# Gated sum and final norm on GpSimd and ScalarE, with another write-back plan, in a macaron decoder layer

## What is computed

```python
h = x
h = h + 0.5 * swiglu(rmsnorm(h, ffn1_norm), ffn1_w_gate, ffn1_w_up, ffn1_w_down)   # D_FF = 2816
u = rmsnorm(h, mix_norm)
a_val, a_gate, b_B, b_C, b_x, g_a, g_b = split(u @ w_in)                           # 7 x 1024 columns
a = silu(layernorm(causal_depthwise_conv(a_val * sigmoid(a_gate), 31 taps) + bias))
y_a = a @ a_w_out
y_b = (b_B * causal_depthwise_conv(b_C * b_x, 3 taps)) @ b_w_out
m = sigmoid(g_a) * y_a + sigmoid(g_b) * y_b
h = h + m @ w_o
h = h + 0.5 * swiglu(rmsnorm(h, ffn2_norm), ffn2_w_gate, ffn2_w_up, ffn2_w_down)
out = rmsnorm(h, final_norm)
```

## Time and profile before

| | us |
|---|---|
| runs: median (lowest to highest of 3) | 3187.16 (3183.77 to 3187.34) |
| profiled execution, its own time | 3187.8 |
| its span, slowest core (the 8: 3170.6 to 3186.2) | 3186.2 |
| PE busy | 3058.0 (96%) |
| DVE busy | 2464.7 (77%) |
| ACT busy | 872.9 (27%) |
| POOL busy (DMA issue only) | 191.1 (6%) |
| DMA moved | 618.14 MB, mean 194 GB/s |

### The profile page before, as it was taken

The page is one execution under the profiler, slowest core; times in us unless marked ns, Lnnn a source line. Parts: engine busy times, 40 slices in busy tenths (PEclk is TensorE's granted clock), DMA queues, the critical chain, the costliest instruction groups (busy, mean ns, idle before and its releaser), DMA issues.

```text
span 3186.2 us, 45381 instructions; the slowest of 8 cores (3170.6 to 3186.2 us)
## 1 busy us (share of the span) xinstructions
PE 3058.0 (96%) x14160; PEld 1386.8 (44%) x14160; DVE 2464.7 (77%) x3458; ACT 872.9 (27%) x1570; POOL 191.1 (6%) x363
## 2 busy tenths in 40 slices
PE   7988899999998999998999999999999999999997
PEld 2433344444443443443444444444444444444445
DVE  2268898869887697958898699989897899897332
ACT  1122233223321223313242233322421332232221
POOL 1111001000110000000000000000001000000000
PEclk9999999999999999999999999999999999999998
DMA  9999989988999779796565656554657545645454
GB/s 178 137 211 198 221 226 176 224 219 212 185 206 248 225 184 241 206 258 210 162 204 171 199 185 207 195 176 154 212 148 231 164 156 184 216 147 197 145 186 158
DMA packets 184649, 618.14 MB, mean 194 GB/s; under 512 B 21024, under 2 KB 23200, under 8 KB 178656
## 3 DMA queue, kind: packets, MB, share of 16 engines
q1 hardware_dynamic: 137024, 440.20, 43.9%
q0 software_dynamic: 45872, 172.78, 28.4%
q10 hardware_dynamic: 1520, 2.27, 0.2%
HBM read 622.50 MB, written 103.81 MB: 228 GB/s over the span
## 4 chain that ended last, share of the span: by engine, by line
PE 78%; DMA 18%; issue 1%; DVE 1%; SPq 1%; ACT 0%; DVEq 0%; POOL 0%; ACTq 0%; POOLq 0%
PE ps L412 78%; DMA wslot<-wpack 7%; DMA wbf<-wslot 5%; DMA hst<-hs 2%; DMA hs<-hst 1%; DMA vecs_sb<-vecs 1%; DMA outT<-hT 1%; DVE acc L412 1%; SPq L412 1%; DMA hT<-hs 0%; DMA wslot<-wbf 0%; DMA hs<-hT 0%; DVE hT L412 0%; DVE rstdX L412 0%; ACT fp L412 0%
## 5 line engine op out<-in xcount | busy, mean ns | idle before, releaser
L412 DVE SCALAR_TENSOR_TENSOR acc<-abuf,vecs_sb,acc 128x512 f32<-128x512 f32 x1920 | 1435.6, 749 | 133.9 <-ACT acc L412 9.6
L412 PE MATMUL ps<-uF,wslot 128*128 128x512 bf16 x5632 | 1255.1, 381 | 39.0 <-DMA wslot<-wpack 20.6
L412 PEld LDWEIGHTS ps<-uF,wslot 128*128 128x128 bf16 x5632 | 550.9, 98 | 719.6 <-issue 70.5
L412 PE MATMUL ps<-uM,wslot 128*128 128x512 bf16 x3584 | 800.0, 380 | 14.8 <-DMA wslot<-wpack 10.3
L412 PE MATMUL ps<-act,wslot 128*128 128x512 bf16 (+1 forms) x2992 | 631.4, 368 | 19.0 <-DMA wslot<-wpack 10.1
L412 ACT ACTIVATE fp<-ps 128x512 f32<-128x512 f32 x513 | 303.4, 595 | 1135.4 <-PE ps L412 1083.9
L412 PEld LDWEIGHTS ps<-uM,wslot 128*128 128x128 bf16 x3584 | 350.4, 98 | 443.8 <-issue 27.1
L412 PEld LDWEIGHTS ps<-act,wslot 128*128 128x128 bf16 x2992 | 292.9, 98 | 341.5 <-issue 30.4
L412 DVE TENSOR_TENSOR act<-fp,ps 128x512 bf16<-128x512 f32 x352 | 239.3, 682 | 213.0 <-PE ps L412 202.3
L412 ACT ACTIVATE sq<-hT 128x512 bf16<-128x512 f32 (+1 forms) x260 | 158.1, 612 | 584.8 <-DVE hT L412 563.0
L412 PE MATMUL ps<-acc,wslot 128*128 128x512 bf16 x1024 | 242.9, 384 | 0.7 <-DMA wslot<-wbf 0.7
(11 more groups left out here) (46 smaller groups left out, 933.6 us busy)
## 6 DMA issues: line engine op xcount, KB each, us to landing
wslot<-wbf SPq DMA_DIRECT2D x480, 512.0 KB, 4.7
wslot<-wpack POOLq DMA_DIRECT2D x160, 512.0 KB, 15.3
wslot<-wbf SPq DMA_DIRECT2D x208, 352.0 KB, 3.4
wbf<-wslot SPq DMA_DIRECT2D x80, 512.0 KB, 11.3
wslot<-wpack POOLq DMA_DIRECT2D x64, 352.0 KB, 11.2
hst<-hs POOLq DMA_DIRECT2D x57, 256.0 KB, 6.0
outT<-hT POOLq DMA_DIRECT2D x14, 1024.0 KB, 7.7
wslot<-wbf SPq DMA_DIRECT2D x48, 256.0 KB, 3.7
```

Of the source, the lines that this page charges most:

```text
L412: ins = getattr(E, meth)(*a, **kw)
```

## The change

1. `_setup`: the load of `vecs` is issued ahead of the four chunks of x; the halving of the taps moves in DVE's list from ahead of the first norm's squares to behind the first normalisation (`halve_taps`).
2. `SLACK_S`: the planner takes chunk loads to land later (side 0: 10/5 us, side 1: 8/4 us, where it was 6/2.5 us for both).
3. `write_use`: which use of a slab writes it back (0 first, 1 second, 2 third). FFN1: the first for every sixth slab (4 `gu1`, 3 `dn1`), else the second. FFN2: the second, as before. Mixer slabs: the third for each index with remainder 1 by 3 (8 `win`, 5 `m3`, 1 `wo`), else the second. `w_land`, the planner's estimate, follows.
4. `last_down`: e = 1 goes from d = 7 down to 0 and its first four groups (8 slabs) use the slabs that e = 0 left in the slots.
5. `final_store`: per chunk a product on POOL and one on ACT in place of one on DVE, each chunk put off until the planner's POOL clock allows; the stores stay on POOL.
6. Gated sum on POOL in place of DVE. The planner takes 1600 ns for each POOL instruction (`POOL_NS`).

```diff
+POOL_NS = 1600.0
-SLACK_S = {True: 6000.0, False: 2500.0}
+SLACK_S = {(0, True): 10000.0, (0, False): 5000.0, (1, True): 8000.0, (1, False): 4000.0}
@@ _setup
+        tr.dma("act", "misc", self.b_vecs, Buf(None), self.vecs[:], self.vecs_d[:], kb=164)
         for k in range(0, KC, 2):
...
-        tr.dma("act", "misc", self.b_vecs, Buf(None), self.vecs[:], self.vecs_d[:], kb=164)
...
-        tr.op("dve", lambda E: E.tensor_scalar_mul(out=self.vecs[:, V_ADW:V_ADW + 8 * CA],
...
+    def halve_taps(self):
+        self.tr.op("dve", lambda E: E.tensor_scalar_mul(out=self.vecs[:, V_ADW:V_ADW + 8 * CA],
...
@@ gen_b
         self.u_left = self.normalize(self.b_h[0], self.b_uF, V_FFN1, n, now=True)
+        self.halve_taps()
@@ slab_at
-    def write_back_first(self, kk):
-        return False
+    def write_use(self, kk):
+        if kk[0] in ("gu1", "dn1"):
+            return 0 if kk[1] % 6 == 0 else 1
+        if kk[0] in ("gu2", "dn2"):
+            return 1
+        return 2 if kk[1] % 3 == 1 else 1
-                if c >= 1 or self.write_back_first(kk):
+                if c == self.write_use(kk):
                     self.slot_dirty[s] = kk
@@ last_down
-            for d in range(KC):
+            for n, d in enumerate(range(KC) if e == 0 else reversed(range(KC))):
+                tk = t + (1 if e == 1 and n >= 4 else 0)
@@ final_store
-            self.scale_op(h[k], h[k], V_FINAL, k, norm)
+            rstd = norm.get()
+            tr.op("pool", lambda E: E.tensor_tensor(out=h[k].ap, in0=h[k].ap, in1=rstd.ap, op=ALU.mult),
+                  reads=[h[k], rstd], writes=[h[k]], cost=POOL_NS)
+            tr.op("act", lambda E: E.activation(out=h[k].ap, in_=h[k].ap, func=AF.Copy,
+                                                scale=self.vecs[:, V_FINAL + k:V_FINAL + k + 1]),
+                  reads=[h[k], self.b_vecs], writes=[h[k]], cost=720)
...
+            if k + 1 < KC:
+                self.defer(tr.t["pool"], lambda: scale(k + 1))
@@ merge_out
-            tr.op("dve", lambda E: E.tensor_tensor(out=mm[i].ap, in0=tt[0].ap, in1=tt[1].ap, op=ALU.add),
-                  reads=tt, writes=[mm[i]], cost=684)
+            tr.op("pool", lambda E: E.tensor_tensor(out=mm[i].ap, in0=tt[0].ap, in1=tt[1].ap, op=ALU.add),
+                  reads=tt, writes=[mm[i]], cost=POOL_NS)
```

More of the change, by code:

```diff
@@ L535, in stage_load @@
         self.tr.dma(self.hq(), "sld%d" % i + self.hq(), b, self.b_hs[t][k], self.stage[i][:], self.hs[t, :, k, :], kb=256,
-                    slack=SLACK_S[self.b_pos <= CAST_POS])
+                    slack=SLACK_S[side, self.b_pos <= CAST_POS])
         r = Ref(b, b.gen)
@@ L552, in w_land @@
         c = self.n_used.get(kk, 0)
[L553 removed]
+        w = self.write_use(kk)
+        nbytes = ne * 128.0 * (4.0 if c < w else (6.0 if c == w else 2.0))
         if not commit:
@@ L954, in last_down @@
             nps = self.bank(hold=True)
-            for d in range(KC):
-                yield ("d", lambda: max(tr.ready(self.b_act), self.w_ready(t + e, "dn2", 2 * d)))
-                sb0, st0 = self.slab(t + e, "dn2", 2 * d)
-                sb1, st1 = self.slab(t + e, "dn2", 2 * d + 1)
+            for n, d in enumerate(range(KC) if e == 0 else reversed(range(KC))):
+                tk = t + (1 if e == 1 and n >= 4 else 0)
+                yield ("d", lambda: max(tr.ready(self.b_act), self.w_ready(tk, "dn2", 2 * d)))
+                sb0, st0 = self.slab(tk, "dn2", 2 * d)
+                sb1, st1 = self.slab(tk, "dn2", 2 * d + 1)
                 ps = self.bank()
@@ L974, in last_down, with stat @@
                       reads=[x], writes=[sq], cost=410)
-                def stat(d=d, sq=sq, nps=nps):
+                def stat(n=n, sq=sq, nps=nps):
                     tr.op("pe", lambda E: E.matmul(nps.ap[:, 0:H], lhsT=self.ones[:], rhs=sq.ap[:, 0:H],
-                                                   start=(d == 0), stop=(d == KC - 1)),
-                          reads=[self.b_ones, sq], writes=([nps] if d == 0 else []), cost=MM_NS / 2)
+                                                   start=(n == 0), stop=(n == KC - 1)),
+                          reads=[self.b_ones, sq], writes=([nps] if n == 0 else []), cost=MM_NS / 2)
                     nps.w = ("pe", tr.cnt["pe"])
@@ L982, in last_down @@
                 self.late.append((tr.ready([sq]), stat))
-                if e == 1 and d == 0:
+                if e == 1 and n == 0:
                     self.flush(tr.ready([sq]) - 1.0)
@@ L1023, in scale, with store, begin @@
         def scale(k):
-            self.scale_op(h[k], h[k], V_FINAL, k, norm)
-            if k % 4 == 3:
-                dst = self.outT[t, :, k - 3:k + 1, :]
-                tr.dma("pool", "ost%d" % p, self.b_out, h[k - 3], dst, self.hT[p][:, k - 3:k + 1, :],
-                       extra_reads=h[k - 2:k + 1], kb=1024)
+            rstd = norm.get()
[4 more added lines that the diff above has]
+                  reads=[h[k], self.b_vecs], writes=[h[k]], cost=720)
+            if k % 4 == 3:
+                self.defer(tr.ready([h[k]]), lambda: store(k))
+            if k + 1 < KC:
+                self.defer(tr.t["pool"], lambda: scale(k + 1))
+        def store(k):
+            dst = self.outT[t, :, k - 3:k + 1, :]
+            tr.dma("pool", "ost%d" % p, self.b_out, h[k - 3], dst, self.hT[p][:, k - 3:k + 1, :],
+                   extra_reads=h[k - 2:k + 1], kb=1024)
             if k == KC - 1:
                 self.stored[q] = tr.ready([], h)
-        self.push_hi([(747.0, lambda k=k: scale(k), lambda k=k: tr.ready([h[k], norm.get()]) if norm.done else INF)
-                      for k in range(KC)])
+        def begin():
+            if norm.done:
+                scale(0)
+            else:
+                self.defer(tr.t["pe"] + 1000.0, begin)
+        self.defer(tr.t["pe"] + 3000.0, begin)
     def win_group(self, tile, c, u):
```

4 lines of the change are left out of this document (2 added, 2 removed).

## The result

| | before | after |
|---|---|---|
| runs: median (lowest to highest of 4), us | 3187.01 (3183.77 to 3187.34) | 3218.51 (3215.79 to 3219.6) |
| ratio of the two (95% interval) | | 1.0099 (1.0083 to 1.0115) |
| span of the profiled execution, us | 3186.2 | 3217.8 |

A forecast was written before the change was run, and what follows sets the result against it. PE was taken to bound from 1510 us to the end, the DMA side up to 395 us. The sum was 3187.8 - 15 + 4 - 6 + 0 + 2 = 3173 us, range 3162 to 3182, chance 0.50.

The forecast's parts named there:

- Parts 5 and 6: Gated sums and final norms: moving DVE work to POOL and ACT, at 1.6 us per POOL instruction, costs +2 us.
- Rival A: Gated sums and final norms: POOL's instructions hold DVE back, each costing DVE its length; 3187 to 3236 us, chance 0.22.
- 1.1 us of hold: DVE beside POOL: below about this hold per POOL instruction, the time stays within the forecast's range.
- Part 1: Kernel start: PE's first weight product comes at about 22 us instead of 33.4, 11.5 us sooner.
- "0.5 us": Kernel start: loading 164 KB of vectors ahead of x delays x by 0.5 us, at 315 GB/s, hidden under the slab.
- Part 3 and the idle DMA time up to 395 us: Stage up to 395 us: 6.4 us of idle DMA time plus 8.4 us less FFN1 slab traffic, about 15 us earlier.
- Part 3, mixer slabs: 814 to 1360 us: 42 us more traffic at the third tile, about a tenth showing, +4 us; bounds 0 and +17.
- Rival C: Third tile: the traffic moved there returns as stalls, +17 instead of +4; 3192 us, 3182 to 3195 around it, chance 0.15.
- Part 2: Two gaps where DVE waits for `hst` chunks: later planned landings take 4 and 2.5 us, -6 us; bounds +5 and -18.
- Part 4: Kernel end: PE stops at the same place, four and a half groups in, so 0 us; bounds -2 and +1.

The follow-up runs named there:

- e1: The changed kernel with gated sum and final norm back on DVE; 0.9927 (0.9904 to 0.995) of the kernel before, 23 us faster.
- e5: The kernel before, order unchanged, with 120 POOL sums on a scratch tile that nobody reads; 1.0106 (1.0071 to 1.0141) of the kernel before.
- e6: The kernel before, order unchanged, with three unread POOL memsets in each of 120 places; 1.008 (1.005 to 1.0111) of the kernel before.
- e11: The kernel before with every transfer of h on SP's queue and 120 unread POOL sums; 1.0014 (1.0001 to 1.0027) of the kernel before.
- e10: The kernel before with every transfer of h on SP's queue and three unread POOL memsets in each of 120 places; 0.9958 (0.9941 to 0.9975).
- e7: The kernel before with the tap halving moved behind the first normalisation, vectors still loaded behind x; 0.9965 (0.995 to 0.998), 11 us faster.
- e4: The kernel before with the change's write-back plan only, FFN1 and mixer slabs; 0.9983 (0.997 to 0.9995), 5 us faster.
- e14: The kernel before with the FFN1 part of the write-back plan only, mixer slabs as before; 1.0039 (1.0022 to 1.0057), 12 us slower.
- e8: The kernel before with only the new `SLACK_S` values; 1.0279 (1.024 to 1.0318), 89 us slower.
- e15_best: The changed kernel without POOL's sum and norm, h on SP, vectors behind x, first half's four output stores on POOL; 0.9861 of the kernel before.

## Why the prediction was wrong, point by point

**Parts 5 and 6, "+2 us": the step that failed.** It cost the two moves as if POOL's instructions lay beside DVE's for nothing, and took that DVE would do the rest unchanged. Shown instead: they cost 55 us (`e1` against the change), and DVE's taps are held (`e5` against `e6`), which by the price in `e11` against `e10` is about 29 of the 55; the rest stays open. The 1.6 us for one POOL instruction was right, 1564 and 1489 ns on average. The Trainium skill's ratio of 1.96 (GPSIMD Engine Reference, section 3.1) had given an estimate of 1.34 us; the trace has 1564/686 = 2.28 and 1489/745 = 2.0, and as the shortest of each 1256 and 1254 ns.

**Rival A was this mechanism**, with 0.22. Its range, 3187 to 3236, holds the 3218.5. But two of its steps were off, in opposite directions. DVE doesn't lose the whole length of every POOL instruction: 81 us for 120 instructions are 0.67 us each, 0.44 of POOL's 182 us (72 of it in the taps); DVE instructions that read PSUM aren't held. Where POOL's products follow each other and DVE has only taps, it loses far more, 9.5 us beside one final norm (1003.29 above). And the point from which it decides, 1.1 us of hold, was too high: 0.67 us on average was enough. By A's own sums 1.1 us comes to (8.8 - 6.9) x 7 = 13 us more, 3186, which is already above the forecast's 3182. That threshold let each tile begin with four full banks and with DVE on time. The 5.51 us stop above shows a sum and a final-norm product right behind each other, and ACT in order behind POOL, which the threshold left out. That A's range holds the time is in part luck: the other terms came out some 7 us better than forecast, and part of the 55 us isn't the hold.

The rule I had beside rival A, in the Trainium skill (SBUF - State Buffer, "Who interferes with whom"), is that a DVE instruction with two SBUF inputs and a GpSimd instruction that reads SBUF exclude each other, while one that only writes does not. The trace agrees in the kind: 765 ns with sums, 748 with memsets, and no change for DVE instructions with one input in PSUM. I should have given it more than 0.22: the argument against it was only that no row showed a hold, and in that trace POOL had no row that could.

**Part 1, PE's start at 22 us: measured 27.15.** The failed term is "0.5 us" for the vectors ahead of x. Timeline of the start after:

```profile
1.06 0.42 ACTq L413 DMA_DIRECT2D vecs_sb<-vecs  x1
...
14.79 0.67 POOL L413 DMA_DIRECT2D wslot<-wpack  x1 [14.09 <-DMA hT<-xT]
...
20.57 0.63 ACT L413 ACTIVATE sq<-hT 128x512 bf16<-128x512 f32 x1 [5.19 <-DMA hT<-xT]
...
27.15 0.38 PE L413 MATMUL ps<-uF,wslot 128*128 128x512 bf16 x1 [1.37 <-DVE uF L413]
```

The last chunk of x is there at 20.5 us instead of 12.1, 8.4 us later, and the first cast goes out at 14.79 instead of 7.28. The DMA issues of the first 34 us have the vectors' own time to landing:

```profile
vecs_sb<-vecs ACTq DMA_DIRECT2D x1, 164.0 KB, 8.6
```

I had divided 164 KB by the mean rate of the queue. The trace of before held the sign: there the vectors, with all of x already there, landed 9.4 us behind its last chunk (12.1 to 21.5). The halving was right: without the vectors first (`e7`) PE starts at 23.4.

**Part 3 and the idle DMA time up to 395 us, -15: right, and too small.** After is 25.4 us ahead at matmul 1432, though it started only 6.8 us ahead. `e1`, whose lists are the same up to 528 us, is 19.8 ahead, so 6 us of it are a matter of the chip or the execution; `e4`, with the plan alone, is 14.3. PE's waits for casts in 160 to 395 fell from 28.4 us to (total, times, longest):

```profile
PE ps L413 <- DMA wslot<-wpack: 17.1, 15, 2.8
```

**Part 3, mixer slabs, +4 of 0 to 17.** `e4` gives back 9.0 us between matmuls 1432 and 6332, twice the term and within its bounds. Rival C named the traffic; `e14` speaks against that as the whole cause, so the mechanism of the term stays open.

**Part 2, -6 us: half of it not seen in the change.** The DVE wait of 10.57 us and PE's 11.68 us became, in the timelines of DVE and PE,

```profile
946.44 0.75 DVE L413 SCALAR_TENSOR_TENSOR uM<-hst,vecs_sb,rstdM 128x512 bf16<-128x512 f32 x1 [16.72 <-DMA hst<-hs]
...
954.25 0.59 PE L413 MATMUL ps<-sq,ones 128*128 128x512 bf16 x1 [17.80 <-ACT sq L413]
```

while in `e1_rest_only` the same gap is 4.6 us, and the last gap, 6.48 us at 2480, is in neither. Alone (`e8`) the slacks took 1.75 and 2.73 us of the two gaps, where 4 and 2.5 were forecast, and then the plan ran out of FFN work. My bounds of +5 and -18 looked at the gaps, and not at what the planner has left at the end.

**Part 4, 0 us: right.** PE stops in the same place for 6.01 us (8.31 before), four and a half groups into e = 1, behind the two stores on SP:

```profile
3193.69 1.65 PE L413 MATMUL ps<-act,wslot 128*128 128x256 bf16 x7 [6.01 <-DMA wslot<-wbf]
```

That the stores hold it is shown by `e15_best`, where they aren't on SP and the stop is gone.

**The sum.** Without the POOL parts my terms come to 3171 us; `e1`, by its ratio of 0.9927, is 3164. The rest of the forecast held as a sum of misses both ways, which is luck; the one term that decided was POOL's.

## What to carry to other kernels

Moving elementwise work from a busy DVE to GpSimd isn't relief by itself: what DVE sheds (82.9 us here) can come back as longer DVE instructions, so compare DVE's total busy time and the mean and longest ns of its commonest group before counting any gain. An engine that gets compute also gets waits in its list, so look first at which DMAs stand in that list. A small transfer, placed ahead of the data that everything waits for, is to be priced by when it landed in the trace, not by its bytes. And a stage is to be compared over several cores: at one mark the cores of one execution differed by up to 25 us here.

## What the runs showed that I had not expected

- 361 memsets on POOL of 525 ns each hold no DVE tap (748 ns), but cost 26 us as long as POOL also issues h's transfers, and nothing (0.9958 against 0.9957) when SP issues them. Moving h to SP gains 14 us by itself.
- The 164 KB of vectors took 8.6 us at the head of a queue (issued at 1.06 us), about the time by which x came later (8.4 us).
- The scratch sum, one tile read as both inputs, took 1260 ns on average and 1027 at the shortest; the real ones, with two tiles, 1564 and 1489 ns, at the shortest 1256 and 1254.
- In the changed kernel PE's stop of 5.5 us is followed by 3.4 or 6.8 us at the 1.2 GHz level on all eight cores, so such a stop costs more than its length. The shorter stops there, of 2.0 to 3.5 us, are on some cores and not on others: the one of 2.35 us on the slowest core only.
- A change of a few constants (`SLACK_S`) moved the end by 89 us with no change of the work, by running out of FFN products beside the last mixer.
